# Gate stage: sums of squares behind the first tiles; attention: both heads' scores issued together

## What is computed

```
y = y * silu(x @ w_z);  y = y * rsqrt(mean of y^2 over groups of 512 features + eps) * ssd_norm_w
o = o * rsqrt(mean of o^2 over each head's 128 features + eps) * hg_norm_w * silu(x @ w_g)
```

```
scores = q @ k.T + causal_mask;  prob = exp(scores - max);  out += (prob * gate / sum(prob)) @ v
```

## Time and profile before

| | |
|---|---|
| median of 3 runs | 3239.78 us (3237.27 to 3256.98) |
| profiled execution | 3237.45 us, span 3235.7 us |
| PE busy | 2765.5 us (85%), 16142 matmuls |
| DVE busy | 1647.4 us (51%) |
| ACT busy | 1094.6 us (34%) |
| mean granted TensorE clock | 0.901 of full |
| gate stage | 793 to 959 us of the span |
| attention stage | 2363 to 2540 us of the span |

### The profile page before, as it was taken

One profiled execution on the slowest core, in us unless ns is written; L12 is line 12 of the kernel. 1 busy time (PEld: TensorE's weight loads), 2 busy tenths in 40 slices (PEclk: granted clock), 3 DMA queues, 4 the chain that ended last, 5 costly groups with the idle time before them and its releaser, 6 DMA issues. The chain is left out here.

```text
span 3235.7 us, 42068 instructions
## 1 busy us (share of the span) xinstructions
PE 2765.5 (85%) x16142; PEld 2155.9 (67%) x16142; DVE 1647.4 (51%) x2591; ACT 1094.6 (34%) x1800; POOL 79.4 (2%) x93
## 2 busy tenths in 40 slices
PE   6979899756889999999969999957699846599998
PEld 3734887645668788776537887847566636478886
DVE  3535222676244788538976886341324363444432
ACT  3322100354232655224335553220134120245531
POOL 0034000000000000000000000000000000000000
PEclk9989999966889999999979999977779967799999
DMA  8723132001133233311112333231200100223332
GB/s 293 252 84 130 53 85 58 13 4 28 40 95 88 85 97 97 106 57 52 40 52 59 98 96 100 63 104 31 59 1 1 48 1 2 65 85 96 92 98 71
DMA packets 373891, 241.00 MB, mean 74 GB/s; under 512 B 7792, under 2 KB 345584, under 8 KB 373744
## 3 DMA queue, kind: packets, MB, share of 16 engines
q1 hardware_dynamic: 373744, 238.96, 24.8%
HBM read 236.31 MB, written 2.10 MB: 74 GB/s over the span
## 5 line engine op out<-in xcount | busy, mean ns | idle before, releaser
L1086 DVE SCALAR_TENSOR_TENSOR ffn_acc<-ffn_pad,cols_sb,ffn_acc 128x512 f32<-128x512 f32 x380 | 263.8, 747 | 32.6 <-ACT ffn_acc L1013 32.6
L223 PE MATMUL bank<-ffn_x_high,pre_high 128*128 128x512 f32 x528 | 212.0, 401 | 14.2 <-DVE ffn_x_low L475 10.7
L224 PE MATMUL bank<-ffn_x_low,pre_high 128*128 128x512 f32 x528 | 210.6, 399 | 0.0
L225 PE MATMUL bank<-ffn_x_high,pre_low 128*128 128x512 f32 x528 | 210.5, 399 | 0.0
L223 PE MATMUL bank<-ffn_x_high,ffn_w_high 128*128 128x512 f32 x528 | 205.5, 389 | 0.0
L225 PE MATMUL bank<-ffn_x_high,ffn_w_low 128*128 128x512 f32 x528 | 205.5, 389 | 0.0
L224 PE MATMUL bank<-ffn_x_low,ffn_w_high 128*128 128x512 f32 x528 | 205.4, 389 | 0.0
L223 PE MATMUL bank<-ffn_h_high,ffn_down_w_high 128*128 128x512 f32 x480 | 190.4, 397 | 0.5 <-DVE ffn_h_low L882 0.5
L224 PE MATMUL bank<-ffn_h_low,ffn_down_w_high 128*128 128x512 f32 x480 | 189.6, 395 | 0.0
L225 PE MATMUL bank<-ffn_h_high,ffn_down_w_low 128*128 128x512 f32 x480 | 188.6, 393 | 0.0
L687 ACT ACTIVATE ffn_down_w_high<-ffn_down_ring 128x1408 fp32r<-128x1408 f32 (+1 forms) x45 | 60.5, 1345 | 212.8 <-PE bank L225 187.4
(11 more groups left out here) (744 smaller groups left out, 6389.7 us busy)
## 6 DMA issues: line engine op xcount, KB each, us to landing
ada_ring<-in_ada_w SPq DMA_DIRECT2D x48, 1024.0 KB, 7.0
pre_ring<-in_ffn_w_up SPq DMA_DIRECT2D x88, 512.0 KB, 3.9
pre_ring<-in_ffn_w_in SPq DMA_DIRECT2D x44, 512.0 KB, 3.9
ffn_down_ring<-in_ffn_w_down SPq DMA_DIRECT2D x28, 704.0 KB, 4.5
ffn_down_ring<-in_ffn_w_out SPq DMA_DIRECT2D x14, 704.0 KB, 4.4
pre_ring<-in_conf_w SPq DMA_DIRECT2D x18, 512.0 KB, 5.0
f_ring<-in_mix_w_in SPq DMA_DIRECT2D x32, 256.0 KB, 3.0
pre_ring<-in_mix_w_in SPq DMA_DIRECT2D x16, 512.0 KB, 3.9
```

The costliest lines, as they stand in the source:

```text
L223: pe.matmul(bank, weights[0], acts[0], start=start, stop=False)
L224: pe.matmul(bank, weights[0], acts[1], start=False, stop=False)
L225: return pe.matmul(bank, weights[1], acts[0], start=False, stop=stop)
L1086: dve.scalar_tensor_tensor(out=dst, in0=src, scalar=conv_w(2 * i + j, n), in1=dst, op0=ALU.mult, op1=ALU.add).then_inc(tapped[j], 1)
```

## The change

In the gate stage all 8 tiles of squares get a place of their own (`br_sq` grows from 4 tiles to 8), so ACT no longer waits for counts before it squares. ACT takes the high parts of the first two slabs ahead of the squares. PE begins with product 0; four `o_count` stand behind product 0 and four behind product 1. The roots of `o` are made at step 2 instead of 1, and PE spreads them behind products 3 to 6 instead of 2 to 5, so in the same step in which DVE scales. `invert` comes first in its DVE step.

In attention the unit of PE's queue becomes a pair of units (both heads, number q). The two score matmuls are issued one right after the other into different banks; the masking matmul is kept for head 0 only, and stands behind both; for head 1, DVE adds the mask in the bank before it takes the maximum. PE issues the scores of pair q + 2, then the two turns of pair q. Scores have four banks now, `turn` banks 4 and 5, `values` bank 6 alone. Four matmuls of 512 columns whose result nobody reads stand in PE's queue between the first two pairs of scores and the loop.

```diff
-    with core.room(br_sq=[P, 4, SEQ], ...
+    with core.room(br_sq=[P, DT, SEQ], ...
...
-            return {1: 0, 6: 1, 10: 2}.get(s - shift)
+            return {2: 0, 6: 1, 10: 2}.get(s - shift)
...
-            for k in range(DT):
-                o_count(k)
             for s in range(slabs):
                 product(s)
-                if 2 <= s < 6:
-                    for k in range(2 * (s - 2), 2 * (s - 1)):
+                if s < 2:
+                    for k in range(4 * s, 4 * s + 4):
+                        o_count(k)
+                if 3 <= s < 7:
+                    for k in range(2 * (s - 3), 2 * (s - 2)):
                         o_root_out(k)
...
+            take_high(0)
+            take_high(1)
             for k in range(DT):
-                if k >= 4:
-                    act.wait_ge(o_counted, k - 3)
-                act.activation(sq[:, k % 4, :], o[:, k, :], ACT.Square).then_inc(o_squared, 1)
-                if k in (3, 7):
-                    take_high(k // 4)
+                act.activation(sq[:, k, :], o[:, k, :], ACT.Square).then_inc(o_squared, 1)
...
-                    act.wait_ge(o_counted, DT)
-                    if s >= 5:
-                        act.wait_ge(y_counted, s - 4)
+                    act.wait_ge(o_counted, s)
...
             for s in range(slabs):
+                if stage_at(s, 1) is not None:
+                    invert(stage_at(s, 1))
                 take_low(s + 2)
...
-    depth, lag = 6, 4
+    depth, lag = 6, 2
...
+            def scores(q):
+                p, t, _ = units[2 * q]
+                branch = pairs[p][1]
+                if q >= 2:
+                    pe.wait_ge(exp_done, 2 * (q - 1))
+                for e in range(2):
+                    rows = slice(HD * e, HD * e + HD)
+                    mm = pe.matmul(score_bank(2 * q + e)[:, 0:width(2 * q)], branch.q[rows, t * P:(t + 1) * P],
+                                   branch.k[rows, 0:width(2 * q)], start=True, stop=not by_pe(e))
+                    if not by_pe(e):
+                        mm.then_inc(scored[e], 1)
+                for e in range(2):
+                    if by_pe(e):
+                        pe.matmul(score_bank(2 * q + e)[:, t * P:(t + 1) * P], ident[:, :], masked[:, :], start=False, stop=True)\
+                          .then_inc(scored[e], 1)
...
+            for q in range(lag):
+                scores(q)
+            for n in range(4):
+                pe.matmul(banks[7][:, :], core.const("ident"), core.const_sb[:, 0:TT, :].rearrange("p n q -> p (n q)"),
+                          start=True, stop=True)
+            for q in range(n_q):
+                if q + lag < n_q:
+                    scores(q + lag)
+                for e in range(2):
+                    turn(2 * q + e)
+                after(2 * q + 1)
...
+            for q in range(n_q + lag):
+                if q < n_q:
+                    for u in (2 * q, 2 * q + 1):
+                        act.wait_ge(top_done, u + 1)
...
+                if q >= lag:
+                    for u in (2 * (q - lag), 2 * (q - lag) + 1):
+                        take(u)
...
+                    dve.wait_ge(scored[e], q + 1)
+                    if not by_pe(e):
+                        last = score_bank(u)[:, t * P:(t + 1) * P]
+                        dve.tensor_tensor(last, last, core.const("neg_since"), ALU.add).then_inc(masked_out, 1)
+                        dve.wait_ge(masked_out, q + 1)
+                    dve.tensor_reduce(top[:, u:u + 1], score_bank(u)[:, 0:width(u)], AX_X, ALU.max, negate=True).then_inc(top_done, 1)
+                if q:
+                    finish(q - 1)
```

More of the change, by code:

```diff
@@ L2678, in o_count @@
                 pe.wait_ge(o_squared, k + 1)
[L2679 removed]
+                count(o_counts, k * TT, sq[:, k, :]).then_inc(o_counted, 1)
             def y_count(k):
@@ L2874, in probs, with score_bank, by_pe @@
             return prob[:, u % depth, 0:width(u)]
+        def score_bank(u):
+            return banks[u % 4]
+        def by_pe(e):
+            return e == 0
+        scored = [scored0, scored1]
         @block.tensor
         def _(pe):
-            def scores(u):
-                p, t, e = units[u]
+            def scores(q):
+                p, t, _ = units[2 * q]
                 branch = pairs[p][1]
[L2881 to L2887, removed]
+                if q >= 2:
[10 more added lines that the diff above has]
+                          .then_inc(scored[e], 1)
             def turn(u):
@@ L2899, in values @@
                 n_tile, branch = pairs[p]
-                bank = banks[5 + n_tile % 2]
+                bank = banks[6]
                 first = p == 0 or pairs[p - 1][0] != n_tile
@@ L2927, in after @@
                     values(u // UNITS - 1)
-                if u % UNITS == 2 and u // UNITS - 2 in ends:
+                if u % UNITS == 3 and u // UNITS - 2 in ends:
                     count(ends[u // UNITS - 2])
             pe.wait_ge(masks_in, 2)
[L2932 to L2937, removed]
+            for q in range(lag):
[9 more added lines that the diff above has]
+                after(2 * q + 1)
             values(len(pairs) - 1)
@@ L3004, in lift @@
                 dve.wait_ge(summed, p + 1)
-                dve.tensor_copy(mix[:, tiles[n_tile][0], :], banks[5 + n_tile % 2][:, :]).then_inc(lifted, 1)
+                dve.tensor_copy(mix[:, tiles[n_tile][0], :], banks[6][:, :]).then_inc(lifted, 1)
             dve.tensor_copy(ident[:, :], core.const("ident")).then_inc(masks_in, 1)
             dve.tensor_copy(masked[:, :], core.const("neg_since")).then_inc(masks_in, 1)
[L3009 to L3014, removed]
-                    lift(ends[u // UNITS - 2], u // UNITS - 2)
+            for q in range(n_q):
+                t = units[2 * q][1]
+                for e in range(2):
+                    u = 2 * q + e
+                    dve.wait_ge(scored[e], q + 1)
[6 more added lines that the diff above has]
+                    finish(q - 1)
+                if 2 * q % UNITS == 0 and 2 * q // UNITS - 2 in ends:
+                    lift(ends[2 * q // UNITS - 2], 2 * q // UNITS - 2)
             finish(n_u // 2 - 1)
```

35 lines of the change are left out of this document (14 added, 21 removed).

## The result

| | before | after |
|---|---|---|
| median, beside each other on one chip | 3238.90 us (3237.27 to 3256.98, 4 runs) | 3163.34 us (3160.81 to 3167.22, 4 runs) |
| ratio, 95% interval | | 0.9756 [0.9725, 0.9787] |
| profiled span | 3235.7 | 3159.0 |
| first high part of the gate stage to the end of product 15 | 798.58 to 951.76: 153.2 | 798.15 to 918.23: 120.1 |
| first scores of attention to its root spreads | 2363.16 to 2531.88: 168.7 | 2329.14 to 2452.83: 123.7 |

Most executions of the kernel before lie near 3239 or near 3258 us, at a mean granted clock of 0.900 or 0.895; its profiled one, at 0.901, is of the first kind.

A forecast was written before the change was run, and what follows sets the result against it. PE bounds both stages: waits and half clock in the gate stage, its own work, then the clock, in attention. 3237.45 - 36 (gate stage) - 42 (attention) = 3159.5 for the profiled execution; forecast 3160, range 3148 to 3184.

The forecast's parts named there:

- Waits of PE for the spreads: Gate stage: PE's idle 4.1, 3 x 3.8 and 7.1 us ahead of spreads go, but for 0 to 0.5 at s = 11.
- Product 0 seven us earlier: Gate stage: product 0 starts at 801.0 instead of 808.0, with 6.9 us of counts now between products.
- The term of 3.4: Gate stage: clock loss from two runs of one-column counts between products, bounds 0 to 6.8 us, middle taken.
- Rival E: Slower: the clock stays at half in both stages, gate stage plus 58 us, attention plus 32, total 3327; chance 3%.
- Score pairs: Attention: two score matmuls on different row halves overlap fully, saving 2.93 us; a round costs 3.2 us less, nine rounds 29.
- DVE's addition and the new wait: Attention: 36 mask additions at 0.28 us each; PE waits 1.1 us once a round, its turn standing behind `take`.
- The clock in attention: Attention: full clock from about 8 us in, instead of 41 us at half; 13 us won, bounds none or 17.
- the four idle matmuls: Start of attention: four unread matmuls, like the dense products behind 808.0, bring the full clock back, delaying the first turn about 2.
- What would show it: Signs: high parts 5.4 to 8.9 us apart, at most two half-clock stretches behind the gate stage's start, attention rounds 12 to 13.

The follow-up runs named there:

- e7: The changed kernel with one count of o behind each eighth of product 1, not four each behind products 0 and 1: 3158.52 us, ratio 0.9728.
- e5: The changed kernel with head 0's masking matmul between the two score matmuls, so they cannot overlap: 3206.49 us, 0.9881 of the kernel before.
- e8: The changed kernel with ACT alternating exp and take head by head in attention, instead of both exps first: 3157.73 us, 0.9732 of the kernel before.
- e3: The changed kernel without the four matmuls that nobody reads: 3162.97 us, 0.9758 of the kernel before.
- e4: The kernel before with only the four unread matmuls added, behind the second score of attention: 3245.54 us, ratio 1.0000.
- e1: The kernel before with only the gate stage of the change, attention as before: 3210.33 us, ratio 0.9915.
- e11: The changed kernel with four counts ahead of product 0, four inside product 1, and ACT alternating exp and take: 3148.75 us, 0.9693 of the kernel before.
- e9: The changed kernel with four squares and counts ahead of product 0, two counts each behind products 0 and 1: 3154.94 us, ratio 0.9708.

## Why the prediction was right, and where it was not

**The total**: 3160 forecast, 3163.34 measured, in the range. The profiled execution had 78 forecast and lost 76.7. Right mostly by its own terms, and nearer than these by some luck: the gate stage gave 33.5 instead of 36, attention 45.0 instead of 42, 0.5 came between them, and 2.3 were given back that no term had.

**Waits of PE for the spreads**: right. All of the earlier trace rows went, the slack at s = 3 was 2.1 us (forecast 1.5), and where the forecast left 0 to 0.5 at s = 11, one weight load waits 0.3.

**Product 0 seven us earlier**: the time was right (800.52 for 801.0) and the credit wrong. I counted the counts at 6.9 behind the products and the early start at 7, an even trade, and then added the clock as a bound of 0 to 6.8 with 3.4 taken. It measured 4.8. With it the terms give 801.0 + 1.8 + 87.0 + 6.6 + 9.5 + 6.9 + 4.8 = 917.6; measured 918.23. The term of 3.4 was mis-sized by 1.4 and is most of the 2.0 by which product 15 ended later than 912.8 + 3.4; e7, where it is zero, ends at 913.73 against 912.8. The nearest row for "thin counts and the clock" was counts that began out of idle time; that counts following dense products with no gap bring the clock down as well, it did not show. Rival E leaned on dense products raising the clock "within 3.4 us each time"; that was read from one place (808.0 to 811.4). Behind the second four counts the clock came back at 828.3, 5.7 us into product 2, and the forecast's own have two stretches of 10 us at half.

**Score pairs**: right. Rows of the recurrent mixer on 32 partitions carried over to 64 partitions and different banks; a round costs 3.3 less, forecast 3.2, and e5, which gives up the overlap alone, pays 2.2 a round. It no longer has the waits of the same round of the change, 0.69 for `take` and 0.23 for the diagonal; 2.2 + 0.9 is 3.1, near the 2.93 for which the overlap stood in the sum. The Trainium skill (TensorE: Matmul & The Clock Gate, "Measured speedup vs the span model") gives 3.07 for four tiles, and by an estimate from it 8 us would have been lost here. 1.06 us for both heads against 1.05 for one shows none of that.

**DVE's addition and the new wait**: right. 0.289 us against 0.28, and 0.52 to 0.93 in eight of the nine rounds against 1.1, at the place named. The Trainium skill (TensorEngine Tiling, "PSUM Bottleneck") warned that copying out of the banks may be next; the trace agrees for that one pair of four, and e8 shows that the order of ACT's queue, not its amount of work, made it late.

**The clock in attention**: the number was near (13 forecast; 29.6 of the 45.0 are PE's work, 15.4 are left), the reason wrong. The failed step is "the four idle matmuls ... resemble the products that brought it back". In the profiled stage after the clock never fell (in seven other runs with this loop it did, for 3.4 us); I had 4 of 19 us lost and 2 of delay. At stake were 41 x 0.47 = 19, and the matmuls took 3.65 of PE's time: 19.3 - 3.65 = 15.6. e3 shows that without them the clock comes back by itself, e4 that with them the loop of before loses it again, e5 that the new loop loses it too once its scores no longer pair up. I had explained the 126 us at full clock in the earlier trace rows by the first `values` and took the state for stable; it was not.

**Given back**: 2.3 us behind attention, at a mean clock of 0.87 instead of 0.88:

```profile
2452.83:3159.00 706.17, 577.15 (x4100) 471.29 (x4100) 301.47 (x394) 210.77 (x282) 7.28 (x6) 0.87 0.22 64
```

The sum had no such term. Nothing there was changed, PE has 4100 records in both. The sum of its stretches at half is 180 us instead of 175, and 5.4 x 0.47 is 2.5, so the clock accounts for all of it; that it falls at other moments because everything lies 79 us earlier is my reading and not tested. e1's attention gave back 4 in the same way. I know no way to forecast its sign.

**What would show it**: the high parts were to come 5.4 to 8.9 us apart; behind the counts they stood 10.7 and 12.3 apart (808.20, 818.86, 831.11). Two half stretches behind the start was the upper of what was named. No spread waits, no late fall of the clock in attention, rounds of 12.1 to 13.3 where 12 to 13 was said.

Open: why the clock fell at 2394.9 of e5 and not a round earlier, behind nearly the same work. The runs show what stood ahead of the falls, not what would have been enough to avoid them.

## What to carry to other kernels

Issue matmuls that use different halves of the rows directly one after the other, with masks and everything else behind both: here it halved their time, and as the denser loop also kept its clock, the gain was twice the arithmetic (20 + 22 us, the second in one execution). Put a spread behind the product of the very step in which its consumer stands, instead of a step ahead of it in a queue that then waits. Put work of one or two columns into time in which PE waits anyway, or singly between dense matmuls; a run of four counts between two dense products was paid again in the clock here (4.8 us for two such runs). Try matmuls that only warm the clock with and without: here they were worth nothing. And let a forecast carry a few us of doubt for stages that are only moved in time: 2.3 and 4 us here.

## What was not expected of the hardware

- The granted clock fell to half while PE had no gap: 17.1 us at 2394.9 of e5 (10.00 of 10.00 us busy ahead), 20.5 at 2468.8 of e4. Ahead of the fall stood 64-row scores, turns of one or two blocks and a count of two columns.
- Four counts in a row (3.65 and 4.03 us of one-column matmuls in the trace) between dense products: half for 3.4 and 6.8 us. Single counts of 0.8 between groups of three dense matmuls (e7) or six (e11), and two in a row (e9): none.
- Two matmuls of 512 columns on rows 0 to 63 and 64 to 127, in two banks: 1.06 us for both, 1.05 for one.
- An addition in place in a bank, 128 x 128: 0.289 us, hardly dearer than an operation from a bank to elsewhere (0.281).
